# Decay logarithms of a state-space layer clamped by ScalarE instead of VectorE, and the products of two heads issued in turn

## What is computed

```python
a_dt = dt_c * a                       # negative, per head and token
a_cs = jnp.cumsum(a_dt, axis=-1)
decay = jnp.exp(jnp.where(causal, a_cs[l] - a_cs[s], -jnp.inf))
cb = jnp.einsum('lgn,sgn->gls', c_c, b_c)
y_diag = jnp.einsum('gjls,sgjp->lgjp', cb * decay, x * dt)
```

## Time and profile before

| | us |
|---|---|
| median of three runs | 1255.05 |
| the three runs | 1255.55, 1246.02, 1255.05 |
| the profiled execution's own time | 1246.88 |
| its span, first to last instruction | 1245.2 |
| mean granted TensorE clock, as a share of full speed | 0.977 |
| busy: TensorE / VectorE / ScalarE / GpSimd | 1166.7 / 828.3 / 649.4 / 189.6 |

### The profile page before, as it was taken

One profiled execution on the slowest core, in us unless ns is written; L12 is line 12 of the kernel. 1 busy time (PEld: TensorE's weight loads), 2 busy tenths in 40 slices (PEclk: granted clock), 3 DMA queues, 4 the chain that ended last, 5 costly groups with the idle time before them and its releaser, 6 DMA issues.

```text
span 1245.2 us, 23675 instructions
## 1 busy us (share of the span) xinstructions
PE 1166.7 (94%) x8884; PEld 1100.9 (88%) x8884; DVE 828.3 (67%) x1237; ACT 649.4 (52%) x976; POOL 189.6 (15%) x141
## 2 busy tenths in 40 slices
PE   5978888899999999958988999999999999999998
PEld 5868878889999999846657999999998899999998
DVE  5999999986866555444654766555667668666553
ACT  5555665545555443346764555444554565555432
POOL 2333333331700000112220100000000211000000
PEclk9999988899999999988999999999999999999999
DMA  6533333338555555422221655555544456555553
GB/s 230 178 120 120 119 126 124 123 105 237 169 172 180 171 169 182 146 78 85 85 69 36 201 185 185 186 184 181 176 152 135 136 171 192 181 185 185 186 185 101
DMA packets 53368, 190.83 MB, mean 153 GB/s; under 512 B 5936, under 2 KB 7088, under 8 KB 53312
## 3 DMA queue, kind: packets, MB, share of 16 engines
q1 hardware_dynamic: 51552, 183.48, 45.3%
q0 software_dynamic: 1760, 6.59, 1.8%
HBM read 188.96 MB, written 1.08 MB: 153 GB/s over the span
## 4 chain that ended last, share of the span: by engine, by line
PE 76%; DVE 15%; issue 4%; ACT 3%; DMA 1%; POOL 1%; DVEq 1%; SPq 0%; ACTq 0%; POOLq 0%
PE lin L410 23%; PE lin L412 22%; PE lin L411 22%; DVE cv L1237 3%; DVE dd L1256 3%; DVE w_lo L1167 2%; PE lin L633 1%; PE lin L631 1%; PE ps L495 1%; PE ps L675 1%; PE ps L674 1%; DMA w_raw<-w 1%; PE ps L748 1%; DVE u L1225 1%; PE ps L771 1%
## 5 line engine op out<-in xcount | busy, mean ns | idle before, releaser
L1167 DVE TENSOR_TENSOR w_lo<-w_raw,w_hi 128x1024 fp32r<-128x1024 f32 (+1 forms) x304 | 373.7, 1231 | 251.4 <-ACT w_hi L816 250.8
L816 ACT ACTIVATE w_hi<-w_raw 128x1024 fp32r<-128x1024 f32 (+2 forms) x344 | 356.0, 1040 | 262.4 <-PE lin L412 258.5
L410 PE MATMUL lin<-x_hi,w_hi 128*128 128x256 f32 (+1 forms) x1528 | 449.0, 294 | 16.5 <-DVE w_lo L1167 11.2
L412 PE MATMUL lin<-x_hi,w_lo 128*128 128x256 f32 (+1 forms) x1528 | 441.5, 289 | 0.0
L411 PE MATMUL lin<-x_lo,w_hi 128*128 128x256 f32 (+1 forms) x1528 | 441.2, 289 | 0.0
L410 PEld LDWEIGHTS lin<-x_hi,w_hi 128*128 128x128 f32 x1528 | 295.1, 193 | 20.8 <-DVE w_lo L1167 11.6
L411 PEld LDWEIGHTS lin<-x_lo,w_hi 128*128 128x128 f32 x1528 | 294.4, 193 | 1.7 <-issue 1.0
L412 PEld LDWEIGHTS lin<-x_hi,w_lo 128*128 128x128 f32 x1528 | 295.2, 193 | 0.0
L412 PE MATMUL lin<-hid_hi,w_lo 128*128 128x256 f32 (+1 forms) x768 | 218.2, 284 | 0.0
L411 PE MATMUL lin<-hid_lo,w_hi 128*128 128x256 f32 (+1 forms) x768 | 217.9, 284 | 0.0
L410 PE MATMUL lin<-hid_hi,w_hi 128*128 128x256 f32 (+1 forms) x768 | 217.4, 283 | 0.0
(11 more groups left out here) (250 smaller groups left out, 1545.1 us busy)
## 6 DMA issues: line engine op xcount, KB each, us to landing
w_raw<-w SPq DMA_DIRECT2D x344, 512.0 KB, 3.3
acs_bc<-acs_dram POOLq DMA_DIRECT2D x8, 544.0 KB, 4.8
bias_mask<-rpb POOLq DMA_DIRECT2D x4, 512.0 KB, 9.6
h<-h SPq DMA_DIRECT2D x4, 272.0 KB, 6.2
out<-h SPq DMA_DIRECT2D x8, 128.0 KB, 3.3
cst<-const SPq DMA_DIRECT2D x1, 784.0 KB, 8.0
vecs<-vec SPq DMA_DIRECT2D x1, 131.5 KB, 2.2
acs_dram<-y POOLq DMA_DIRECT2D x1, 34.0 KB, 3.7
```

The costliest lines, as they stand in the source:

```text
L410: mm3(o, wh, xh, start=first and i == 0, stop=False)
L412: ins = mm3(o, wl, xh, start=False, stop=last and i == kts - 1)
L816: a(w_hi[pg.slot][:, 0:n], w_raw[pg.slot][:, 0:n], ACT.Copy).then_inc(w_hi_done, 1)
L1167: tt(w_lo[pg.slot][:, 0:n], w_raw[pg.slot][:, 0:n], w_hi[pg.slot][:, 0:n].bitcast(F32), ALU.subtract)\
```

## The change

The twelve clamps of a group go from VectorE to ScalarE, as relu(column - row), which is the clamped logarithm with its sign turned; the exponential then takes a scale of -1, and the columns are stored without the negation. ScalarE issues them behind its first two `hi` of a slot and ahead of `decay`. At the start ScalarE waits for one more memset. In `y_products` the two heads of a pair alternate piece by piece instead of one head after the other, and the wait for `mm_done` is made once.

```diff
-                    for e in range(2):
-                        j = 2 * q + e
-                        pe.wait_ge(mm_done, g.times(2, q + 1).value)
-                        rows = slice(e * HD, (e + 1) * HD)
-                        cs = slice(j * HD, (j + 1) * HD)
-                        nc.tensor.matmul(o[rows, 0:T], x_tok[:, 0, cs], mm[:, j, 0:T], start=True, stop=False)
-                        nc.tensor.matmul(o[rows, 128:T], x_tok[:, 1, cs], mm[:, j, T:416], start=False, stop=False)
-                        ins = nc.tensor.matmul(o[rows, 256:T], x_tok[0:META, 2, cs], mm[0:META, j, 416:432],
-                                               start=False, stop=True)
+                    pe.wait_ge(mm_done, g.times(2, q + 1).value)
+                    halves = [(slice(e * HD, (e + 1) * HD), 2 * q + e) for e in range(2)]
+                    for rows, j in halves:
+                        nc.tensor.matmul(o[rows, 0:T], x_tok[:, 0, j * HD:(j + 1) * HD], mm[:, j, 0:T],
+                                         start=True, stop=False)
+                    for rows, j in halves:
+                        nc.tensor.matmul(o[rows, 128:T], x_tok[:, 1, j * HD:(j + 1) * HD], mm[:, j, T:416],
+                                         start=False, stop=False)
+                    for rows, j in halves:
+                        ins = nc.tensor.matmul(o[rows, 256:T], x_tok[0:META, 2, j * HD:(j + 1) * HD],
+                                               mm[0:META, j, 416:432], start=False, stop=True)
...
-            act.wait_ge(memset_done, 4)
+            act.wait_ge(memset_done, 5)
...
+            def decay_logs(g, half):
+
+                if half == 0:
+                    act.wait_ge(acs_in, (g + 1).times(16).value)
+                    if g.base == 0:
+                        act.wait_ge(cols_done, 4)
+                    else:
+                        act.wait_ge(ee_done, g.times(2).value)
+                for j in (2 * half, 2 * half + 1):
+                    h_at = g.times(4, j)
+                    for s, (rows, at, n, l0) in enumerate(((P, 0, T, 0), (P, T, 144, 128), (META, 416, 16, 256))):
+                        ins = a(dd[0:rows, j, at:at + n], acs_bc[0:rows, j, l0:T], ACT.Relu, scale=-1.0,
+                                bias=cols[0:rows, 3 + s, bass.ds(h_at.value, 1)])
+                ins.then_inc(dd_done, 1)
...
-                a(ee[:, hs, :], dd[:, hs, :], ACT.Exp).then_inc(ee_done, 1)
+                a(ee[:, hs, :], dd[:, hs, :], ACT.Exp, scale=-1.0).then_inc(ee_done, 1)
...
                 if has_scan:
+                    decay_logs(g, 0)
+                    decay_logs(g, 1)
                     decay(g, 0)
                     decay(g, 1)
...
-                for i, sign in ((0, 1.0), (3, -1.0)):
-                    ts(cols[:, i:i + 2, :], src[:, i:i + 2, :], sign, None, ALU.mult).then_inc(cols_done, 1)
-                    ts(cols[0:META, i + 2, :], src[0:META, i + 2, :], sign, None, ALU.mult).then_inc(cols_done, 1)
+                for i in (0, 3):
+                    nc.vector.tensor_copy(cols[:, i:i + 2, :], src[:, i:i + 2, :]).then_inc(cols_done, 1)
+                    nc.vector.tensor_copy(cols[0:META, i + 2, :], src[0:META, i + 2, :]).then_inc(cols_done, 1)
...
-            def log_decays(g, half):
...
-                    log_decays(g, 0)
-                    log_decays(g, 1)
```

More of the change, by code:

```diff
@@ L1184, in _ @@
             dve.memset(dd[:, :, 416:432], 0.0)
-            dve.memset(cbm[:, 416:432], 0.0)
+            dve.memset(cbm[:, 416:432], 0.0).then_inc(memset_done, 1)
             dve.wait_ge(vec_in, 16)
```

## The result

The change makes the kernel slower by 0.37%: the ratio of its times to those of the kernel before is 1.0037, 95% interval 1.0020 to 1.0055 (medians of twenty runs each 1253.93 and 1249.52 us). The forecast was 1257.0 on a shown median of 1255.05, so within 1%, and slightly slower; so it came out. The means of the runs are 4.7 us apart, and of the two parts that make up this difference only one was forecast, as follows.

What follows compares the result with a forecast made beforehand. VectorE was taken to bound the SSD layer's intervals. First statistic -1.9, five intervals +7.7 and last two groups' products -3.3 gave +2.5 us, 1257.6 on the median, stated as 1257.0; range 1240 to 1273.7, likeliest 1249 to 1264.

Steps and rivals of the forecast that it cites:

- What bounds before: SSD layer: VectorE sets the pace, busy 29.21 of 30.80 us; TensorE's only real wait is for `cbm`.
- The clamps' price: On ScalarE: 0.90 us a head, 3.6 a group, bounds 3.0 to 4.5.
- Their place: Clamps behind ScalarE's second `hi`: `conv0` starts at t0+7.1, the statistic comes at t0+14.3, TensorE waits some 6.5 us.
- t0: Point in an interval between statistics where TensorE's first chunk ends and the transposes begin.
- The products: TensorE's products of two heads, 4.24 us a group before, were taken to overlap when alternated, saving 1.66 us.
- rival B: The array doesn't overlap the heads, S between 0 and 0.36: +11.6 to +14.1 us, middle 1268; chance 0.26.
- S: Saving per group from alternating two heads' products on TensorE: bounded by nothing and 2.1 us, taken as 1.66.
- The interval: Statistic to statistic in the SSD layer: 14.3+19.2-1.66 us each; five make 159.2 against 151.5, +7.7.
- VectorE's load: VectorE's busy time in an interval falls by the clamps' 6.7 us, from 29.2 to about 22.5.
- Rival A: VectorE was the bound and gives all back: intervals of some 24.5 us, 1220 on the median; chance 0.12.
- The sum: Over slots 1 to 8 of the SSD layer: -1.9+7.7-3.3 = +2.5 us on the profiled 1246.88.
- Rival C: TensorE's clock doesn't fall after the gap: 2.1 us less per interval, -10.5 in all, 1247; chance 0.09.

Runs made afterwards that it cites:

- e1: The kernel before with only the products of two heads alternating, clamps still on VectorE: 1252.47 us, ratio 1.0007.
- e4: The kernel after with `conv0` moved ahead of the clamps on ScalarE, directly behind the slot's two roundings: 1235.02 us, ratio 0.9877.
- e6: The kernel after without the clamps of every second head, whose logarithms stay zero: 1240.19 us, ratio 0.9939.
- e5: As e4, with ScalarE's square also moved ahead of the clamps: 1244.94 us, ratio 0.9961.
- e11: As e4, with ScalarE's square between the clamps and the exponentials: 1237.69 us, ratio 0.9907.
- e13: The kernel before, clamps on VectorE, with GpSimd's three `w_lo` of a slot moved to VectorE: 1233.47 us, ratio 0.9888.

## Why the prediction was right, and where it was not

- **What bounds before.** Right. e1 shows it: 2.1 us less TensorE work in a group shortens the interval by 0.3 us (30.3 to 30.0), or 0.7 against the second profile of before (30.7), and the wait for `cbm` takes the rest.
- **The clamps' price**: 3.6 us forecast and 0.12 until the exponential; measured 3.67 from the first clamp's start to the exponential's, both in one. No row shows the 0.12, nor the 0.06 of the upper bound for the moving column, and the 3.67 leaves no room for the latter. **Their place**: `conv0` at t0+7.1, measured t0+7.01; the statistic at t0+14.3, measured 14.50; the wait at some 6.5, measured 6.6. e4 (same instructions, `conv0` first, 17.3 us less) and e6 (half of them, 11.6 less) show that this chain closed the loop.
- **The products.** Rightly taken to overlap, which excludes rival B, but S was mis-sized: 1.66 forecast, 2.1 measured, the upper bound. The stagger of one record that I took off doesn't show from start to start: a pair takes 1.07 us, with the next pair behind it (159.95 to 161.02). The Trainium skill's page "TensorE: Matmul & The Clock Gate", section "Part 3: Packing small matmuls — row/col tiling", says that small matmuls placed in different tiles of the array run at the same time, and this trace agrees: 1.07 us for two heads against 1.06 for one.
- **The interval.** 14.3+19.2-1.66 = 31.8 forecast, 31.2 measured. From statistic to t0 16.57+2.1 = 18.7 would be without the overlap, against my 19.2.
- **VectorE's load.** Forecast 22.5 us, measured 26.95. I took all of the clamps as gone, and at 6.7 us where they held VectorE 5.8. A part of them was time behind GpSimd's `w_lo`, and this doesn't go with the instruction that suffers it: `g_lo` now takes 1.56 us in the mean instead of 0.48, VectorE's `w_lo` 1.54 instead of 1.22, a tap 0.87 instead of 0.81, which makes 3.9 us in an interval. What stands ahead of `conv0` (`g_lo`, `w_lo`) costs nothing in this kernel, where VectorE then waits for ScalarE. The long taps behind `conv0` (4.65 us, where e4's take 2.84) do stand on the path; the forecast had them, as part of the 7.17 us of slot 2. The toll limits e4, e5 and e11, and my expectations for them were too good by it. Rival A would have been wrong even with the better order: e4's intervals are 28.6 us, not 24.5.
- **The sum.** In the layer +2.5 was forecast, and -1.3 measured in the profile (-2.5 against the second profile of before). Term by term: the first statistic -2.5, forecast -1.9; the five intervals +4.6, forecast +7.7; from the sixth statistic to the last -3.3, forecast -3.3. So the intervals carry the miss, and 2.2 of their 3.1 us are the mis-sized S. The failed step is the one before the sum: "Behind the SSD layer TensorE is nearly always busy, and nothing of the change is there. So the sum is made over the slots 1 to 8." The attention stage behind it has waits on every head, and its clock differs from kernel to kernel, from 0.94 to 0.85, though nothing in it was edited. The 4.7 us measured are a layer some 2 us shorter and a tail that is longer, by 13 us in the profiles and by less in the mean of the runs. That the time came out right is luck: one of its two parts is missing, and the two errors, +4 in the layer and the absent tail, have opposite signs.
- **Rival B's condition.** "Slower from S below 0.3" is a slip: by the sum, 2.5+7x(1.66-S) passes 12.6 only below 0.22, and with clamps at 3.8 below about 0.4. With S measured at 2.1 nothing hangs on it.
- **Rival C** (the clock stays full in the layer) is wrong. The grant is 0.89 as in the earlier trace rows; but that row is one of the two slowest intervals before, where three of the five had 0.94 to 0.98. Over the five the mean grant falls from 0.93 to 0.88. The forecast has this in its 19.2 us, which it took after long gaps.

## What to carry to other kernels

Work moved to an idle engine isn't free by that engine's busy share: what counts is the instruction that it is put ahead of, and whether another engine waits for that one. The same holds for an instruction that itself waits: put first, it holds up all behind it (e5's square). Before moving work off an engine, look whether its instructions are long or only held up; if they are held up, move what holds them (e13), or the toll passes to the next instruction. And a difference below 1% can come from a stage that the change never touches: compare the stage's end in both traces before the sum is believed, set the profiled run against its kernel's other runs, and delay one kernel by a microsecond or two to see how much the tail moves by itself.

## What the runs showed of the hardware

- Two products of 128x64 into different halves of the PSUM rows, issued in turn, take as long as one: 1.07 us for a pair of heads against 1.06 us for one head.
- A GpSimd subtraction of 128x1024 (2.4 to 2.6 us) holds up VectorE's instructions beside it, in four kinds seen here: twelve clamps 5.79 us against 3.65, six taps take 5.38 us against 2.84, a product of 128x864 3.23 against 1.06, two `g_lo` 3.05, where their mean in the trace of before is 0.48 for each. VectorE itself does that subtraction in 1.22 us (mean of the kernel before).
- In the profiles, 1.7 us of added TensorE work ahead of a stage with many short waits moved its mean grant from 0.94 to 0.84 in one kernel and from 0.83 to 0.88 in the other, with +12.8 and -7.6 us in the tail; in the medians of the runs it was some +10 us and nothing.
